# Two-pass attention values: the rounded part and the rest of a head's values side by side in the stationary tile

## The reference, cut to what matters

```
# first layer: compressed, selected and window parts of each head (4 groups g, 4 heads r each)
o_c = jnp.einsum('bgrqc,bcgd->bqgrd', p_c.astype(v_cmp.dtype), v_cmp)
o_s = jnp.einsum('bgrqt,bgqtd->bqgrd', p_s.astype(vs.dtype), vs)
o_w = jnp.einsum('bgrqk,bkgd->bqgrd', p_w.astype(vw.dtype), vw)
return gb[..., 0:1] * o_c + gb[..., 1:2] * o_s + gb[..., 2:3] * o_w
# second layer: sliding window of 128, 16 heads that share 2 sets of keys and values
o = jnp.einsum('bnhgqs,bnshd->bnqhgd', probs, vb)
```

## Time and profile before

| what | value |
|---|---|
| median of three runs | 2478.98 us |
| profiled execution, its span (first to last instruction) | 2475.2 us |
| mean granted TensorE clock | 0.996 |
| PE busy / weight loads busy | 2431.0 / 2032.8 us, 12006 instructions each |
| DVE busy | 1400.0 us (57%) |
| ACT busy | 975.7 us (39%) |
| POOL busy | 179.2 us (7%) |
| DMA | mean 93 GB/s |

### The profile page before, as it was taken

How to read it: one execution, slowest core, us unless ns; L and a number is a source line. 1 busy time by engine, 2 the same in 40 slices (tenths; PEclk the granted TensorE clock), 3 DMA queues, 4 the chain that set the end, 5 groups by cost and what they waited for, 6 DMA issues and landing times.

```text
span 2475.2 us, 31208 instructions
## 1 busy us (share of the span) xinstructions
PE 2431.0 (98%) x12006; PEld 2032.8 (82%) x12006; DVE 1400.0 (57%) x2842; ACT 975.7 (39%) x1808; POOL 179.2 (7%) x244
## 2 busy tenths in 40 slices
PE   9999999999999999999999999999999998999998
PEld 7888889888887878788888888878888887888887
DVE  6435556676666676675443446667644566543444
ACT  4223334432335565553322334555422345422332
POOL 0000000100002222220000000222200002000000
PEclk9999999999999999999999999999999999999999
DMA  4454443333321111122233333211122431223222
GB/s 151 111 131 131 107 132 123 102 104 110 106 90 52 60 52 60 52 69 94 99 92 104 102 98 124 72 56 53 59 70 94 132 117 67 94 87 109 94 86 93
DMA packets 86380, 231.36 MB, mean 93 GB/s; under 512 B 8488, under 2 KB 23464, under 8 KB 86234
## 3 DMA queue, kind: packets, MB, share of 16 engines
q1 hardware_dynamic: 81072, 221.42, 27.2%
q10 hardware_dynamic: 5162, 7.95, 2.1%
HBM read 217.80 MB, written 11.53 MB: 93 GB/s over the span
## 4 chain that ended last, share of the span: by engine, by line
PE 92%; DVE 4%; ACT 3%; issue 1%; DMA 0%; POOL 0%; DVEq 0%; SPq 0%; ACTq 0%
PE bank L977 90%; PE bank L1190 2%; ACT t_pp L1636 0%; DVE t_pp L2146 0%; ACT t_tmp L1483 0%; ACT t_PS L1483 0%; DVE t_PS L1898 0%; ACT t_whi L1483 0%; PE bank L1364 0%; DVE t_ST L2419 0%; ACT t_pw L1636 0%; DVE t_wlo L1893 0%; DMA t_XT<-in_xT 0%; DVE t_pw L2146 0%; DVE t_CB L2010 0%
## 5 line engine op out<-in xcount | busy, mean ns | idle before, releaser
L977 PE MATMUL bank<-t_XH,t_whi 128*128 128x512 f32 x2064 | 813.2, 394 | 6.0 <-DVE t_sa L2146 3.4
L977 PE MATMUL bank<-t_XH,t_wlo 128*128 128x512 f32 x2064 | 804.4, 390 | 0.0
L977 PE MATMUL bank<-t_XL,t_whi 128*128 128x512 f32 x2064 | 804.1, 390 | 0.0
L1893 DVE TENSOR_TENSOR t_wlo<-t_raw,t_whi 128x1024 fp32r<-128x1024 f32 (+2 forms) x418 | 479.4, 1149 | 363.1 <-ACT t_whi L1483 360.0
L1483 ACT ACTIVATE t_whi<-t_raw 128x1024 fp32r<-128x1024 f32 (+3 forms) x422 | 415.6, 988 | 412.4 <-PE bank L977 357.5
L977 PEld LDWEIGHTS bank<-t_XH,t_whi 128*128 128x128 f32 x2064 | 387.9, 188 | 88.3 <-DVE t_sa L2146 4.5
L977 PEld LDWEIGHTS bank<-t_XH,t_wlo 128*128 128x128 f32 x2064 | 387.8, 188 | 82.1
L977 PEld LDWEIGHTS bank<-t_XL,t_whi 128*128 128x128 f32 x2064 | 388.2, 188 | 77.4
L977 PE MATMUL bank<-t_RX,t_whi 128*128 128x512 f32 x1056 | 325.0, 389 | 0.0
L2010 DVE TENSOR_TENSOR t_tmp<-bank,t_RB 128x512 f32<-128x512 f32 x178 | 122.6, 689 | 222.8 <-PE bank L977 217.8
L977 PEld LDWEIGHTS bank<-t_RX,t_whi 128*128 128x128 f32 x1056 | 198.2, 188 | 41.1
(11 more groups left out here) (321 smaller groups left out, 2740.9 us busy)
## 6 DMA issues: line engine op xcount, KB each, us to landing
t_raw<-in_f_in SPq DMA_DIRECT2D x86, 512.0 KB, 3.2
t_raw<-in_f_out SPq DMA_DIRECT2D x32, 384.0 KB, 3.1
t_raw<-in_w_conv SPq DMA_DIRECT2D x24, 512.0 KB, 3.2
t_raw<-in_w_merge SPq DMA_DIRECT2D x24, 512.0 KB, 3.2
t_raw<-in_fg SPq DMA_DIRECT2D x22, 512.0 KB, 3.2
t_raw<-in_fu SPq DMA_DIRECT2D x22, 512.0 KB, 3.2
t_raw<-in_f_out SPq DMA_DIRECT2D x32, 320.0 KB, 2.9
t_raw<-in_w_g SPq DMA_DIRECT2D x16, 512.0 KB, 3.2
```

What stands on the lines that cost most here:

```text
L977: return e.matmul(o, l, r, start=start, stop=stop, skip_group_check=True)
L1893: e.tensor_tensor(wlo[n % NRAW][:, 0:width], raw[n % NRAW][:, 0:width], f32(whi[n % NHI][:, 0:width]), ALU.subtract).then_inc(*w_lo.tick(n))
```

## The change

The rounded part and the rest of a head's values now stand side by side in one stationary tile, 64 columns each, without zeros. The helper `two` multiplies this tile by the rounded weights and then by the rest of the weights. Partitions 0 to 63 of the bank then hold hi values by both parts, 64 to 127 lo values by both parts. Each head has a bank to itself, and its result is the sum of the two halves: ACT copies the upper half to SBUF (`slow`, `oalow`), DVE adds it to the lower half (`both_halves`). In the sparse stage the sums of a pair go to the two halves of `OC`, from which `smerge` merges; in the window stage to `OC2`, from which `oa` makes `OAH` and `OAL`. These items go through `w.later` in place of standing right behind `values`. The planner's cost of `values` is 6 and 4 in place of 8 and 6. `VS`, `VC` and `VW` shrink, and their zero fills (POOL L2546, DVE L2346) go, but for `VC`.

```diff
-                    own += {"spa": 8, "mem": 12, "win": 6, "mm2": 6}[hd.kind]
-                    w.spent += {"spa": 8, "mem": 12, "win": 6, "mm2": 6}[hd.kind]
+                    own += {"spa": 6, "mem": 12, "win": 4, "mm2": 6}[hd.kind]
+                    w.spent += {"spa": 6, "mem": 12, "win": 4, "mm2": 6}[hd.kind]
...
-            small = {(1, 0): {0: one("cclear", g), 2: one("cscore", g), 3: one("cback", g)},
+            small = {(1, 0): {0: one("cclear", g), 2: both(w.catch_up, one("cscore", g)), 3: one("cback", g)},
...
-                            w.add("smerge", 2 * g + p, w.first_merge(2 * g + p), n)
+                            w.later.append(one("slow", 2 * g + p, n))
+                            w.later.append(lambda: w.add("smerge", 2 * g + p, w.first_merge(2 * g + p), n))
...
+                def after(g=g, r=r, n=len(w.heads) + len(heads)):
+                    w.later += [one("oalow", n), one("oasum", n)]
+                    if r % 2:
+                        w.later.append(one("oa", 2 * g + r // 2))
...
+        def two(o, l, rh, rl, start, stop):
+            mm(o, l, rh, start, False)
+            return mm(o, l, rl, False, stop)
...
-                o = take("ov", ("out", n)) if first else banks[("out", n - q)]
+                o = take("ov", ("out", n)) if a == 0 else banks[("out", n - 1)]
                 for j in range(4):
-                    f = three(o[:, j * P:S], VS[:, a, 0, j, c:c + P], VS[:, a, 1, j, c:c + P],
-                              ph[:, j * S:(j + 1) * S - j * P], pl[:, j * S:(j + 1) * S - j * P], first and j == 0, False)
-                if final:
+                    f = two(o[:, j * P:S], VS[:, a, j, g % 2, :], ph[:, j * S:(j + 1) * S - j * P],
+                            pl[:, j * S:(j + 1) * S - j * P], a == 0 and j == 0, False)
+                if q == 3:
                     operand(("pc", g))
-                    f = three(o, VC[0][:, p, :], VC[1][:, p, :], PCT[0], PCT[1], False, True)
+                    for x in range(2):
+                        f = two(banks[("out", n - 3 + 2 * x)], VC[:, r - 1 + x, :], PCT[0], PCT[1], False, True)
...
+        def oalow(n):
+            on.wait_ge(*full.at(("values", n)))
+            on.wait_ge(*evac.at(("os", n - 2)))
+            copy(OT2[n % 2], banks[("out", n)][64:128, :]).then_inc(*copied.tick(("ot", n)))
+        def slow(m, n):
+            on.wait_ge(*full.at(("values", n)))
+            for x in range(2):
+                on.wait_ge(*evac.at(("os", n - 7 + 2 * x)))
+                copy(OT[x], banks[("out", n - 3 + 2 * x)][64:128, :]).then_inc(*copied.tick(("ot", n - 3 + 2 * x)))
...
         def smerge(m, first, n):
-            on.wait_ge(*full.at(("values", n)))
-            merge(m, 0, first, T[4], ("sgate", m), banks[("out", n - 3)], ("free", ("out", n - 3)))
+            on.wait_ge(*evac.at(("taken", m - 1)))
+            for x in range(2):
+                both_halves(OC[64 * x:64 * x + 64, :], n - 3 + 2 * x, OT[x])
+            on.wait_ge(*evac.at(("os", n - 1)))
+            merge(m, 0, first, T[4], ("sgate", m), OC, ("taken", m))
...
+        def both_halves(o, n, x):
+            on.wait_ge(*copied.at(("ot", n)))
+            e.tensor_tensor(o, banks[("out", n)][0:64, :], x, ALU.add).then_inc(*evac.tick(("os", n), ("free", ("out", n))))
+        def oasum(n):
+            x = (n - WIN0) % 2
+            on.wait_ge(*x_lo.at(("oa", 0, (n - WIN0) // 2 - 1)))
+            on.wait_ge(*x_hi.at(("oa", 0, (n - WIN0) // 2 - 1)))
+            both_halves(OC2[64 * x:64 * x + 64, :], n, OT2[n % 2])
```

More of the change, by code:

```diff
@@ L681, in second_mixer @@
                 more = dict(at={0: prepare}) if r == 0 else {}
-                if r % 2:
-                    more["after"] = lambda g=g, r=r: w.add("oa", 2 * g + r // 2)
+                def after(g=g, r=r, n=len(w.heads) + len(heads)):
+                    w.later += [one("oalow", n), one("oasum", n)]
+                    if r % 2:
+                        w.later.append(one("oa", 2 * g + r // 2))
+                more["after"] = after
                 heads.append(Head("win", 0, range(4), g=g, r=r, **more))
         attend(heads, jobs, 830)
+        w.catch_up()
         w.add("banks", WIDE_OPEN)
@@ L833, in build @@
     TB = [TB4[:, r, :] for r in range(4)]
-    VS = place("VS", 5120, 5120, F32R).rearrange("p (a c j n) -> p a c j n", a=2, c=2, j=4)
+    VS = place("VS", 5120, 2048, F32R).rearrange("p (a j g n) -> p a j g n", a=2, j=4, g=2)
+    OC, OT = place("OC", 7168, 512), [place(f"OT{q}", 7680 + 512 * q, 512)[0:64, :] for q in range(2)]
     PS = place("PS", 10240, 7040, F32R)
     PCT = [place(f"PCT{q}", 17280 + q * 512, 512, F32R) for q in range(2)]
-    VC = [place(f"VC{q}", 18304 + q * 256, 256, F32R).rearrange("p (r n) -> p r n", r=2) for q in range(2)]
+    VC = place("VC", 18304, 512, F32R).rearrange("p (r n) -> p r n", r=4)
     PC = place("PC", 18816, 512).rearrange("p (i c) -> p i c", i=4)
@@ L857, in build @@
     KFT = [place(f"KF{q}", 16896 + 512 * q, 512) for q in range(2)] + [T[4]]
-    VW = place("VW", 17920, 2560, F32R)
-    VS2 = VW.rearrange("p (c j n) -> p c j n", c=2, j=4)
+    VS2 = place("VW", 17920, 1024, F32R).rearrange("p (j g n) -> p j g n", j=4, g=2)
+    OC2, OT2 = place("OX", 18944, 512), [place(f"OY{q}", 19456 + 512 * q, 512)[0:64, :] for q in range(2)]
     OAH, OAL = (place(f"OA{q}", 20480 + q * 4096, 4096, F32R).rearrange("p (k n) -> p k n", k=KD) for q in range(2))
@@ L1209, in values @@
                 g, r, a, p, q = (hd.more[x] for x in "grapq")
[L1210 to L1211 removed]
+                o = take("ov", ("out", n)) if a == 0 else banks[("out", n - 1)]
                 operand(("sv", g // 2, 3))
[L1213 removed]
                 for j in range(4):
[L1215 to L1217 removed]
+                    f = two(o[:, j * P:S], VS[:, a, j, g % 2, :], ph[:, j * S:(j + 1) * S - j * P],
+                            pl[:, j * S:(j + 1) * S - j * P], a == 0 and j == 0, False)
+                if q == 3:
                     operand(("pc", g))
[L1219 removed]
+                    for x in range(2):
+                        f = two(banks[("out", n - 3 + 2 * x)], VC[:, r - 1 + x, :], PCT[0], PCT[1], False, True)
             elif hd.kind == "win":
[L1221 to L1222 removed]
+                g = hd.more["g"]
+                o = take("ov", ("out", n))
                 operand(("va", 1))
[L1224 removed]
                 for j in range(4):
                     wd = 256 if j < 3 else P
[L1227 to L1228 removed]
+                    f = two(o[:, j * P:j * P + wd], VS2[:, j, g // 2, :], ph[:, 256 * j:256 * j + wd],
+                            pl[:, 256 * j:256 * j + wd], j == 0, j == 3)
             else:
@@ L1725, in svs @@
                 on.wait_ge(*full.at(("sv", half, i)))
-                on.wait_ge(*cleared.at("sparse"))
                 if half:
@@ L1792, in qa @@
             stack_q(T[0], T[1], QS2[g % 2][:, 2 * q:2 * q + 2, :], ("qa", g, q))
+        def oalow(n):
+            on.wait_ge(*full.at(("values", n)))
+            on.wait_ge(*evac.at(("os", n - 2)))
+            copy(OT2[n % 2], banks[("out", n)][64:128, :]).then_inc(*copied.tick(("ot", n)))
         def oa(m):
-            n = WIN0 + 2 * m
-            on.wait_ge(*full.at(("values", n + 1)))
-            copy(OAH[:, m, :], banks[("out", n)]).then_inc(*x_hi.tick(("oa", 0, m)))
+            on.wait_ge(*evac.at(("os", WIN0 + 2 * m + 1)))
+            copy(OAH[:, m, :], OC2).then_inc(*x_hi.tick(("oa", 0, m)))
+        def slow(m, n):
[3 more added lines that the diff above has]
+                copy(OT[x], banks[("out", n - 3 + 2 * x)][64:128, :]).then_inc(*copied.tick(("ot", n - 3 + 2 * x)))
         def om(m):
@@ L2281, in svs @@
                     src = banks[("sv", half, i)][:, a * P:(a + 1) * P].rearrange("p (g d) -> p g d", g=2)
-                    hi, lo = (VS[:, a, c, i, 64:320].rearrange("p (g d) -> p g d", g=2)[:, :, 0:64] for c in range(2))
-                    low_scaled(lo, src, norm_r(1)[0][:, i:i + 1], hi, ("sv", half, i), ("free", ("sv", half, i)))
+                    low_scaled(VS[:, a, i, :, 64:128], src, norm_r(1)[0][:, i:i + 1], VS[:, a, i, :, 0:64], ("sv", half, i), ("free", ("sv", half, i)))
         def heads16(x):
@@ L2359, in vas @@
             for g in range(2):
-                hi, lo = (VS2[:, c, :, 64 + 128 * g:128 + 128 * g] for c in range(2))
-                low(lo, src[:, :, g, :], hi, ("va", g), *([("free", ("vat",))] if g else []))
+                low(VS2[:, :, g, 64:128], src[:, :, g, :], VS2[:, :, g, 0:64], ("va", g), *([("free", ("vat",))] if g else []))
         def qa(g, q, n):
@@ L2370, in qa @@
             stack_q(T[0], T[1], QS2[g % 2][:, 2 * q:2 * q + 2, :], ("qa", g, q))
+        def both_halves(o, n, x):
[6 more added lines that the diff above has]
+            both_halves(OC2[64 * x:64 * x + 64, :], n, OT2[n % 2])
         def oa(m):
-            low(OAL[:, m, :], banks[("out", WIN0 + 2 * m)], OAH[:, m, :], ("oa", 0, m), ("free", ("out", WIN0 + 2 * m)))
```

(5 more changed lines are left out.)

25 lines of the change are left out of this document (7 added, 18 removed).

## The result

The changed kernel takes 2493.49 us, the median of four runs (2492.31 to 2494.98), against 2477.91 (2476.45 to 2479.24, four runs) for the kernel before in the same session: ratio 1.0062, interval 1.0050 to 1.0074. It is 15.6 us slower; 2463.9 us had been predicted. The profiled execution, with a device time of 2493.74 us, has a span of 2491.9 us.

A forecast was written before the change was run, and what follows sets the result against it. PE was taken to bound the kernel, busy 98% of the span. Terms -25.4 + 5.5 + 2 + 0.3 + 1 + 1.5 = -15.1 us gave a 2460.1 us span, 2463.9 us as median; range 2454 to 2474.

The forecast's parts named there:

- PE's work less: Values matmuls: 19.8 us less in sparse entries, 7.6 less in window heads, 2.0 more in compressed parts; 25.4 us saved.
- ends: Last merge and low parts of the sparse stage: 0.3 us later; end of the window stage: nothing.
- window stage: Window stage as a whole, with 5 us of PE idle time before: 1 us added.
- The output bank: Next pair's first values want the bank just completed; 7 us of room, so nothing, at worst 1 us at 7 places.
- The start of a group: Compressed scores wait for `T[4]` until the last merge, at three groups: 2 us added, bounds 0 and 8.
- The clock: Lower clock after PE stops in the sparse stage: one more stretch, 1.5 us added, bounds 0 and 5.
- PE's pace: Eight matmuls of a sparse entry start within 1.24 us (twelve took 1.86); a fourth compressed matmul adds 0.25 us to 0.74.
- Rival 2: DVE and ACT bound the sparse stage, swallowing its 17.8 us; only the window stage gains 6.6: 2472.4 us, chance 0.21.
- The bursts: `smerge` grows from two to four DVE operations at eight pair ends: 5.5 us added, bounds 0 and 11.
- Rival 3: At eight pair ends DVE waits for ACT's copies, PE stops and resumes at lower clock: 16 us slower, 2495, chance 0.05.
- Rival 1: All added DVE and ACT work is hidden, the whole 25.4 us gained: 2453.6 us, chance 0.17.
- rival 4: The eight matmuls of a sparse entry take as long as the twelve: 2487 us with the bursts, chance 0.02.

The follow-up runs named there:

- no_sums: The changed kernel without the copies and sums of halves, merge and `oa` reading the even head's bank, result not the layer's: 2463.45 us, 0.9945 of the kernel before.
- load_only: no_sums with two unused DVE operations of 64x512 put back ahead of each of the eight sparse-stage merges: 2468.41 us, 0.9965 of the kernel before.
- act_only: no_sums with two unused ACT copies of 64x512 put back at each of the eight sparse-stage pair ends: 2465.30 us, 0.9948 of the kernel before.
- own_tile: The changed kernel with a tile of its own (CT) for the compressed scores in place of `T[4]`: 2488.58 us, 1.0041 of the kernel before.
- direct: The changed kernel with a pair's copies, sums and merge right behind its values, not in `w.later`: 2482.24 us, 1.0017 of the kernel before.
- one_sum: The changed kernel with tile CT, merge right behind the values, ACT copying both halves, one 128x512 DVE sum per pair: 2487.46 us, 1.0043 of before.
- copies_first: The changed kernel with tile CT, ACT's copies right behind the values, DVE's sums and merge one item later: 2489.79 us, 1.0045 of the kernel before.

## Why the prediction was wrong

The forecast was 15.1 us faster on the span, the outcome about 15.6 slower: 30.7 us. The two stages account for it. Each term as the prediction had it, and what the differences of the stage times gave; the fourth row is a remainder, and holds whatever the others don't:

| term | forecast | measured | by |
|---|---|---|---|
| PE's work less | -25.4 | -14.6 | no_sums: -9.5 and -5.1 |
| DVE's added work at pair ends | +5.5 | +4.4 | load_only against no_sums |
| ACT's copies | 0 | +0.8 | act_only against no_sums |
| bank, `T[4]`, clock, ends | 0 + 2 + 1.5 + 0.3 | +19.5 | what is left of the 24.7 us |
| window stage | +1 | +5.4 | changed against no_sums (4.7 by the means) |
| sum | -15.1 | +15.5 | |

**The output bank: the step that failed.** "The first values of a pair used to wait for a bank given back 16 tiles earlier; now it is the bank of the head just completed ... I cost it at nothing; if the queue is 4 us longer, up to 1 us at each of 7 places." The 7 us of room behind it were read at a group's start, where the next group's compressed scores and their transposition lie between. At three of the four pair changes within a group there are only 2.8 us of PE work (806.42 to the stop), and at the first of them the sum came 5.5 us after the last matmul group. The prediction gave copies and sums 2.5 us at most; with the queues ahead of them the first sum ended 6.2 us after that group. The result: four stops, 9.5 us, and the lower clock behind the two long ones. The room could have been read in the trace before: 2.85 us behind 807.77, 998.13 and 1085.80. The distance to the next values belonged to be read at these narrow places. The prediction had named the sign of its own failure, "a wait of the first values of a pair for a sum (the bank)".

**The start of a group** was right in kind and wrong in size: 2 us, bounds 0 to 8, against 7.6 by own_tile (4.9 by its medians); the waits grew from 1.2 us to 9.7. I had counted the time of the operations and not the queue in front of them. The merge's place in `w.later` came on top: ACT finds `T[4]` taken and PE waits for ACT, up to 4.93 us.

**The clock**: 1.5 us, bounds 0 to 5, against 9.4 (within the 19.5 of the table). I had counted three stretches and one more. The trace before has two, the changed kernel seven: behind the two long stops at the bank, behind the three at `T[4]`, and two more, from 917 and from 1020 us.

**PE's pace** was right: eight matmuls of an entry in 1.21 us (at most 1.24 forecast), four compressed ones in 0.97 (0.74 + 0.25). The Trainium skill ("TensorE: Matmul & The Clock Gate", section "Back-to-back issue gap") would have the eight in about 0.85 us, as an estimate from its 131 and 81 ns with the middle widths between. The trace disagrees for these operands, as before the change. But not all of the work saved becomes time, and that was the second term that failed: 25.4 us counted in full, 14.6 measured. Rival 2 said why: shorter values give each tile less time to get through bias, exponential and scaling. It was half true: 8.3 of 17.8 us in the sparse stage and 2.5 of 7.6 in the window stage are swallowed. I had counted it against that DVE is at 77%. The mean says nothing here, since PE had been waiting for DVE at 70% as well.

**The bursts** (5.5 against 4.4) came out near, with some luck: 5.5 was half of the upper bound, and it holds only for an end at which nothing waits. PE's waits for the bias operation and the low part (L2146 and L1898 before, 10.3 us) are up to 13.2 and not to the 18 that I looked for. Of the wait for ACT I wrote that the late place "lets me count no further wait of DVE for ACT". That was right (2.5 us), and it was bought with the bank and `T[4]`. At once, it is the other way round: nothing for the bank, and up to 5.8 us for the chain over ACT. None of the moves above gets down to no_sums plus the work.

**Rival 3** gave 2495 and a cost of 42 us against 25.4 of gain. The measured costs are 30.1 us plus 10.8 swallowed, 40.9; that the sums agree is in good part luck, since the parts differ. Its four operations, lower clock and group starts are there, its first step (DVE waits for ACT at eight ends) is not: that is direct's and one_sum's. Rival 1 falls by no_sums, which has nothing to hide and takes 2463.45 us, rival 4 by the pace. The 0.05 on rival 3 was too little: "only about half of the places have no slack" counted slack for DVE's work and not for the bank.

What stays open: whether and why copies_first runs at a lower clock than direct with the same idle time; what the wait for the bank alone costs, and what the chain over ACT; why the two operations of load_only cost 4.4 and not the 11.0 of their full time was not followed place by place. A sum of the two halves straight from the bank could have spared copy and wait. It wasn't tried: the Trainium skill ("PSUM — Partial Sum Buffer", section "Specifications (TRN2)") says that a VectorE instruction may take at most one tensor input from PSUM. No run here shows that.

## What to carry to other kernels

When a result needs one more step before its buffer is free, look for the narrowest place where the buffer is wanted again, and count the queues of both engines there, not the time of the operations: here 2.8 us of room stood against 5.5. More buffers are no cure if they come out of the same pool. Price a saving on the bounding engine by leaving the added work out altogether, as no_sums does; if the engine was already waiting for another now and then, part of the saving turns into longer waits. And a chain over two engines that take their work in order can cost more than its operations do: here 11.0 us together, 4.4 and 0.8 alone.

## What the runs showed of the hardware

Half the partitions took DVE and ACT as long as all of them, as the rows of the sums and copies show:

```profile
L2392 DVE TENSOR_TENSOR t_OC<-bank,t_OT x16: 671/683/685, 811.9 to 1125.7; 64x512 f32<-64x512 f32 x16
```

```profile
L1495 ACT ACTIVATE t_OT<-bank x16: 581/589/597, 808.3 to 1124.8; 64x512 f32<-64x512 f32 x16
```

against 0.69 and 0.58 us for 128 partitions. I had not expected what more stops of PE, up to 4.9 us each, do to the clock: seven stretches at the lower level in place of two, 0.96 over the sparse stage, and 9.4 us in all. Nor what one of six banks is worth to the rest of the stage: 15.2 us net in this kernel, though the wait for the output bank went with it.
